# One product per cell from a crossed key plane, in the masked levels of a bidirectional gated recurrence

## The chip, the cores and the metric

The kernel runs on one core of a Trainium2 chip. The metric is the device time of one execution in microseconds (us). TensorE (PE) multiplies, VectorE (DVE) and ScalarE (ACT) work elementwise, GpSimd (POOL) does one kind of subtraction here, and SyncE (SP) issues the transfers. The engines run on their own and meet at semaphores; each takes its instructions strictly in the order in which they are written.

## What is computed

Two layers, each with a feed-forward block before and after a token mixer: the first mixer is latent attention, the second a gated linear recurrence (HGRN2) in both directions over 512 tokens with 8 heads of 128. The change is in the recurrence alone. Per head and direction the reference computes

```python
# S_t = diag(f_t) S_{t-1} + k_t outer v_t ; o_t = S_t^T q_t
diff = where(lower, bt[t] - bt[s], -inf)        # bt: running sum of log f
scores = einsum('bhtd,bhsd,bhtsd->bhts', qt, kt, exp(diff))
o = scores @ vt + einsum('bhtd,bhdv->bhtv', qt * exp(bt), state)
```

so the score of a query t and a key s is a product over 128 channels in which every channel carries the product of the gates between s and t. The two directions are summed.

## The kernel before, in words

**Levels.** The kernel does not scan. It splits the pairs (t, s) by levels m = 1, 2, 4, ..., 256: at level m the tokens stand in blocks of 2m, and a pair belongs to the level if s and t lie in different halves of one block. `k_lev` and `q_lev` (two planes each, one per direction, 128x1024 a plane for the two heads worked on together) hold keys and queries already multiplied by the gates up to the middle of their block. `update(n, m)` on DVE (L1847) brings them from level m to 2m: two products for the queries (L1852), one for the keys (L1854), whose operands `crossed` (L384) walks over the first halves of the blocks in plane 0 and the second halves in plane 1, and one that pairs up the gates (L1857).

**Masked levels.** For m = 1 to 16 the blocks are smaller than the 32x32 cells in which scores are computed. `masked(n, m)` on PE (L909) computes all 32 cells (8 columns of cells, 4 groups of 32 rows) of a level, each as two products: plane d of the keys against those queries of plane 1-d that lie in the other halves, 16 columns each (L919). All five levels write to one PSUM bank. DVE copies what belongs to the level through a mask into `nearest` (`keep`, L1861, instruction L1872). Only after that may the next level overwrite the bank.

**Quarters.** The heads go in four quarters n = 0 to 3 of two heads. While the scores of quarter n are made, the projections of the next quarter run between them. PE's written order around the masked levels is: `masked(n, 1)`, a projection (24 products of 128x512, L554 to L556), `masked(n, 2)`, a projection, and so on up to `masked(n, 16)`, a projection, `within_64` (L932, level 32, one product per cell and 32 columns). In quarters 1 and 2 (counted from 0) some small products stand there too: the sums of squares (L1005) before `masked(n, 2)`, `widen` (L651) before `masked(n, 4)` and `masked(n, 8)`. In the last quarter the output projection takes the place of the projections; it starts from `xg_hi` and `xg_lo`, which ACT (L1436) and DVE (L1892) make of the normed heads.

**DVE's written order** at a masked level of quarters 0 to 2 is: `keep`, `update(n, m)`, `evict()` (L1648, the finished projection times a norm factor into one of three temporaries), `split` (L1605, the low part of a weight tile). **ACT's written order** there is: `gate(n + 1, i)` (L1364 to L1381: four instructions L1375, L1376, L1378, L1380 on the temporary that `evict()` has just made), `hi_part()` (L1171, the high part of a weight tile, 128x1024), and the next gate. The weight tiles go through a ring of four.

The lines that matter here:

```python
# ACT, at the top of the loop over quarters
for n in range(QUARTERS - 1):
    hi_part()
    gate(n + 1, 0)
    hi_part()
    ...
    gate(n + 1, 1)
    hi_part()
# DVE
keep(0, 1)
update(0, 1)
evict()
split(s, t + 5)
keep(0, 2)
```

Of the kernel before, what the change touches and what calls it, by code (L numbers as in the profile page):

```python
# [29 lines left out]
F32 = mybir.dt.float32  # L30
# [3 lines left out]
ACT = mybir.ActivationFunctionType  # L34
ALU = mybir.AluOpType
AX = mybir.AxisListType.X

P = 128
D_MODEL, SEQ, DEPTH, D_FF = 1024, 512, 2, 2816
# [12 lines left out]
SUB = 32  # L52
# [159 lines left out]
def build(nc, x, w_up, w_down, w_mla, w_hgrn, columns, consts, positions, out):  # L212
    ctx = ExitStack()
    with ctx:
        def sb(name, shape, dt=F32):
            return ctx.enter_context(nc.sbuf_tensor(name, shape, dt))

        def sem(name):
            return ctx.enter_context(nc.semaphore(name))
# [20 lines left out]
        t_d = sb("t_d", [P, SEQ])  # L240
        cos = sb("cos", [P, SEQ])
        sin = sb("sin", [P, SEQ])
        eps = sb("eps", [P, 1])
        lb = sb("lb", [P, 2, HEADS])
        one_lb = sb("one_lb", [P, 2, HEADS])
# [119 lines left out]
        act_step = sem("act_step")  # L365
        gate_ready = sem("gate_ready")
        level_ready = sem("level_ready")
        score_done = sem("score_done")
        score_out = sem("score_out")
        near_made = sem("near_made")  # L370
# [13 lines left out]
        def crossed(both, m):  # L384

            start = both[:, 0, :]
            return bass.AP(tensor=start.tensor, offset=start.offset,
                           ap=[list(start.ap[0]), [2 * m, N // (2 * m)], [N + m, 2], [1, m]])

        def runs(n, m):  # L390

# [143 lines left out]
        def _(pe):  # L535
# [42 lines left out]
            def close(instruction):  # L578

                instruction.then_inc(w_free, 1)  # L580
                closed[0] = True
# [287 lines left out]
            def hgrn():  # L869
# [21 lines left out]
                def cell(c, g):  # L891
                    return slice(c * P + g * SUB, c * P + g * SUB + SUB)

                def of_cell(ps, c, g):
                    return ps[g * SUB:(g + 1) * SUB, c * SUB:(c + 1) * SUB]
# [13 lines left out]
                def masked(n, m, closing=False):  # L909

                    ps = open_scores()
                    pe.wait_ge(level_ready, LEVELS_UP * n + m.bit_length())
                    for c in range(CELLS):
                        for g in range(P // SUB):
                            out_c = of_cell(ps, c, g).rearrange("p (b two m) -> p b two m", two=2, m=m)
                            for d in range(2):
                                queries = q_lev[n % 2][:, 1 - d, cell(c, g)]
                                queries = queries.rearrange("p (b two m) -> p b two m", two=2, m=m)
                                last = pe.matmul(out_c[:, :, 1 - d, :], k_lev[n % 2][:, d, cell(c, g)],  # L919
                                                 queries[:, :, 1 - d, :], start=True, stop=True)  # L920
                                if closing and c == g == d == 0:
                                    close(last)
                    last.then_inc(score_done, 1)

                def within_64(n):
# [230 lines left out]
        def _(act):  # L1156
# [9 lines left out]
            def hi_part(blocks=8):  # L1166

                slot = stream.slot()
                act.wait_ge(raw_full[slot], raw_in[slot].next(16))
                n = blocks * P  # L1170
                act.activation(w_hi[slot][:, 0:n], raw[slot][:, 0:n], ACT.Copy).then_inc(hi_made, 1)  # L1171
# [184 lines left out]
            def hgrn():  # L1356
# [8 lines left out]
                def gate(n, i):  # L1365

                    d, j = i // PAIR, i % PAIR
                    at = slice(j * SEQ, (j + 1) * SEQ)
                    head = slice(n * PAIR + j, n * PAIR + j + 1)
                    z = next_temp()  # L1370
                    keys = k_lev[n % 2][:, d, at]
                    if gated.count:
                        act.wait_ge(gate_ready, gated.count)
                    gated.more += 1
                    act.activation(t_c[:, :], z, ACT.Sigmoid).then_inc(act_step, 1)  # L1375
                    act.activation(keys, z, ACT.Sigmoid, scale=-1.0).then_inc(taken, 1)  # L1376
                    act.wait_ge(taken, took.next())
                    act.activation(keys, keys, ACT.Copy, scale=one_lb[:, d, head])  # L1378
                    act.wait_ge(act_step, steps.next())
                    act.activation(gates[n % 2][:, d, at], t_c[:, :], ACT.Identity, bias=lb[:, d, head],  # L1380
                                   scale=one_lb[:, d, head]).then_inc(gate_ready, 1)  # L1381

                def query(j):
                    z = next_temp()
                    took.more += 1
                    act.activation(q_raw[:, j * SEQ:(j + 1) * SEQ], z, ACT.Silu).then_inc(taken, 1)

                def output_gate(n, j):
                    z = next_temp()
                    took.more += 1  # L1390
                    act.activation(y[:, n * PAIR + j, :], z, ACT.Silu).then_inc(taken, 1)

                def unit():
                    act.wait_ge(unit_done, units.next())
                    return psum[:, UNIT_BANKS[(units.count - 1) % 2], :]
# [5 lines left out]
                def nearest_out(n):  # L1401
                    act.wait_ge(score_out, SCORES * (n + 1))
                    for g in range(P // SUB):
                        rows = slice(g * SUB, (g + 1) * SUB)
                        last = act.activation(near[rows, :, rows], nearest[rows, :, :], ACT.Copy)
                    last.then_inc(near_made, 1)
# [26 lines left out]
                def o_hi(head):  # L1433
                    act.wait_ge(chunk_new, normed + head + 1)
                    new.more += 1
                    act.activation(xg_hi[:, head, :], y[:, head, :], ACT.Copy).then_inc(chunk_hi, 1)  # L1436
# [6 lines left out]
                hi_part()  # L1443
                query(0)
                query(1)
                hi_part()
                out_of_psum.more += PAIR
                values_out(0, 0)
# [2 lines left out]
                for n in range(QUARTERS - 1):  # L1451
                    hi_part()
                    gate(n + 1, 0)
                    hi_part()
                    if n:
                        take_root([(0, CELLS, P)], TAIL_BANKS[0])
                    gate(n + 1, 1)
                    hi_part()
                    gate(n + 1, 2)
                    hi_part()  # L1460
                    gate(n + 1, 3)
                    hi_part()
                    query(0)
                    nearest_out(n)
                    hi_part()
                    within_64_out()
                    query(1)
                    hi_part()
                    within_128_out()
                    output_gate(n, 0)  # L1470
                    hi_part()
                    within_256_out()
                    output_gate(n, 1)
                    out_of_psum.more += PAIR
                    hi_part()
                    across_out(0)
                    hi_part()
                    o_out(0)
                    across_out(1)
                    values_out(n + 1, 0)  # L1480
                    o_out(1)
                    values_out(n + 1, 1)

                n = QUARTERS - 1
                hi_part()
                output_gate(n, 0)
                hi_part()
                act.wait_ge(drained, out_of_psum.count + 1)
                o_hi(0)
                take_root([(0, CELLS, P)], TAIL_BANKS[0])  # L1490
                output_gate(n, 1)
                o_hi(1)
                o_hi(2)
                o_hi(3)
                hi_part()
                o_hi(4)
                o_hi(5)
                nearest_out(n)
                hi_part()
                hi_part()  # L1500
# [40 lines left out]
        def _(dve):  # L1541
# [283 lines left out]
            def hgrn(s):  # L1825
# [21 lines left out]
                def update(n, m):  # L1847

                    dve.wait_ge(level_ready, LEVELS_UP * n + m.bit_length())
                    for d in range(2):  # L1850
                        q = pairs(q_lev[n % 2], 1 - d, m)[:, :, 1 - d, :]
                        dve.tensor_tensor(q, q, of_runs(n, d, d, m), ALU.mult)  # L1852
                    k = crossed(k_lev[n % 2], m)
                    dve.tensor_tensor(k, k, crossed_runs(n, m), ALU.mult).then_inc(level_ready, 1)  # L1854
                    if m < P:
                        both = runs(n, m)[:, :, 0:N // m].rearrange("p d (b two) -> p d b two", two=2)
                        dve.tensor_tensor(runs(n, 2 * m)[:, :, 0:N // m // 2], both[:, :, :, 0], both[:, :, :, 1],  # L1857
                                          ALU.mult).then_inc(dve_step, 1)
                        dve.wait_ge(dve_step, step.next())
# [290 lines left out]
```

## Time and profile before

| what | value |
|---|---|
| median of 3 runs | 2126.39 us (2120.18 to 2127.16) |
| profiled execution, own time | 2123.81 us |
| its span | 2122.0 us |
| PE busy | 2077.4 us, 98% of the span |
| PE weight loads | 1703.3 us, 80% |
| DVE, ACT, POOL busy | 897.6, 690.0, 664.9 us |
| mean granted clock of PE | 0.991 |
| the recurrence's stage | about 1370 to 1720 us of the span |

Busy time of PE counts overlapping products once. An fp32 product shows as two records. A time in a row is that of the merged records, from the start of the first to the end of the last, and the last part of a product overlaps the start of the next. Intervals are therefore read from start to start below.

### The profile page before, as it was taken

To read this page: it belongs to the slowest core of one execution; us is meant where nothing else is said; L and a number is where in the kernel's file an instruction comes from. 1 tells how busy PE (TensorE), PEld (TensorE's weight loads), DVE (VectorE), ACT (ScalarE), POOL (GpSimd) and SP (SyncE) were. 2 spreads that over 40 slices of the span, in tenths; PEclk is the share of its full clock that TensorE was granted. 3 is DMA by queue.
4 is the path that set the end of the run, shared out by engine and by line. 5 is a ranking of instruction groups with operands and counts; after the bars stand their busy time and mean duration, and the time that the engine had idled before them with its cause. 6 is when DMAs were issued, how large, how long until landed. Compare 5 with 4: busy or idle time off the path is not lost.

```text
span 2122.0 us, 31462 instructions
## 1 busy us (share of the span) xinstructions
PE 2077.4 (98%) x12734; PEld 1703.3 (80%) x12734; DVE 897.6 (42%) x1223; ACT 690.0 (33%) x930; POOL 664.9 (31%) x286
## 2 busy tenths in 40 slices
PE   8999999989999999999999999999999999999997
PEld 6888888767878888887888888878888778888885
DVE  4433331668464333015433311564755756333213
ACT  4222232445342222223222222453544443222221
POOL 2444444130224444442444444200000013444442
PEclk9999999999999999999999999999999999999998
DMA  4222333210122222332222333221211112222332
GB/s 149 89 90 98 97 92 99 90 50 1 51 89 89 89 98 96 92 99 89 89 92 96 97 92 99 90 72 61 72 61 62 52 70 80 99 92 96 92 102 74
DMA packets 51643, 179.61 MB, mean 85 GB/s; under 512 B 5728, under 2 KB 5984, under 8 KB 51552
## 3 DMA queue, kind: packets, MB, share of 16 engines
q1 hardware_dynamic: 51552, 178.30, 25.9%
q8 instruction: 68, 1.11, 0.2%
q14 instruction: 23, 0.19, 0.0%
HBM read 176.18 MB, written 2.10 MB: 84 GB/s over the span
## 4 chain that ended last, share of the span: by engine, by line
PE 92%; DVE 5%; ACT 2%; issue 1%; DMA 0%; DVEq 0%; SPq 0%; ACTq 0%
PE psum L554 27%; PE psum L556 26%; PE psum L555 26%; PE psum L815 1%; PE psum L791 1%; PE psum L919 1%; PE psum L672 1%; PE psum L666 1%; PE psum L667 1%; DVE xt L1590 1%; DVE xg_lo L1596 1%; PE psum L804 1%; PE psum L968 1%; ACT xg_hi L1214 1%; PE psum L651 1%
## 5 line engine op out<-in xcount | busy, mean ns | idle before, releaser
L504 POOL TENSOR_TENSOR w_lo<-raw,w_hi 128x1024 fp32r<-128x1024 f32 (+1 forms) x282 | 664.7, 2359 | 1426.5 <-ACT w_hi L1171 1426.5
L554 PE MATMUL psum<-xg_hi,w_hi 128*128 128x512 f32 x1758 | 701.1, 399 | 10.9 <-DVE t_a L1648 4.3
L556 PE MATMUL psum<-xg_hi,w_lo 128*128 128x512 f32 x1758 | 690.9, 393 | 0.0
L555 PE MATMUL psum<-xg_lo,w_hi 128*128 128x512 f32 x1758 | 688.0, 391 | 0.0
L1171 ACT ACTIVATE w_hi<-raw 128x1024 fp32r<-128x1024 f32 (+1 forms) x339 | 350.8, 1037 | 839.5 <-DMA raw<-w_up 461.2
L554 PEld LDWEIGHTS psum<-xg_hi,w_hi 128*128 128x128 f32 x1758 | 331.9, 189 | 84.0 <-DVE t_a L1648 6.0
L556 PEld LDWEIGHTS psum<-xg_hi,w_lo 128*128 128x128 f32 x1758 | 331.6, 189 | 76.4
L555 PEld LDWEIGHTS psum<-xg_lo,w_hi 128*128 128x128 f32 x1758 | 331.8, 189 | 70.2
L554 PE MATMUL psum<-hid_hi,w_hi 128*128 128x512 f32 x704 | 273.9, 389 | 0.0
L556 PE MATMUL psum<-hid_hi,w_lo 128*128 128x512 f32 x704 | 273.9, 389 | 0.0
L555 PE MATMUL psum<-hid_lo,w_hi 128*128 128x512 f32 x704 | 273.9, 389 | 0.0
L1648 DVE TENSOR_TENSOR t_b<-psum,r_pre 128x512 f32<-128x512 f32 x100 | 69.1, 691 | 354.0 <-PE psum L556 353.3
L1669 DVE COPY y<-psum 128x512 f32<-128x512 f32 x48 | 33.2, 691 | 399.0 <-PE psum L556 341.1
L555 PEld LDWEIGHTS psum<-hid_lo,w_hi 128*128 128x128 f32 x704 | 132.1, 188 | 27.7
L556 PEld LDWEIGHTS psum<-hid_hi,w_lo 128*128 128x128 f32 x704 | 132.1, 188 | 27.4
L554 PEld LDWEIGHTS psum<-hid_hi,w_hi 128*128 128x128 f32 x704 | 132.1, 188 | 27.4
L1648 DVE TENSOR_TENSOR t_a<-psum,r_pre 128x512 f32<-128x512 f32 x100 | 69.1, 691 | 153.0 <-PE psum L556 132.9
L1655 DVE TENSOR_TENSOR t_d<-t_c,t_b 128x512 f32<-128x512 f32 x88 | 116.4, 1322 | 17.4 <-ACT t_c L1236 6.2
L1236 ACT ACTIVATE t_c<-t_a 128x512 f32<-128x512 f32 x88 | 55.7, 633 | 142.1 <-DVE t_a L1648 142.1
L1605 DVE TENSOR_TENSOR w_lo<-raw,w_hi 128x1024 fp32r<-128x1024 f32 x57 | 69.7, 1223 | 11.6 <-ACT w_hi L1171 10.4
L1659 DVE TENSOR_TENSOR hid_lo<-t_d,hid_hi 128x512 f32 (+1 forms) x88 | 69.3, 787 | 9.4
L666 PE MATMUL psum<-xg_hi,w_hi 128*128 128x512 f32 x138 | 56.2, 407 | 2.7 <-POOL w_lo L504 1.4
(198 smaller groups left out, 1581.7 us busy)
## 6 DMA issues: line engine op xcount, KB each, us to landing
raw<-w_up SPq DMA_DIRECT2D x176, 512.0 KB, 3.3
raw<-w_down SPq DMA_DIRECT2D x64, 512.0 KB, 3.5
raw<-w_hgrn SPq DMA_DIRECT2D x48, 512.0 KB, 3.4
raw<-w_down SPq DMA_DIRECT2D x32, 384.0 KB, 3.1
raw<-w_mla SPq DMA_DIRECT2D x19, 512.0 KB, 3.3
xt<-x_t SPq DMA_DIRECT2D x8, 256.0 KB, 6.6
out<-xt SPq DMA_DIRECT2D x8, 256.0 KB, 2.0
sq<-positions SPq DMA_DIRECT2D x1, 256.0 KB, 9.6
```

The costliest lines, as they stand in the source:

```text
L504: pool.tensor_tensor(w_lo[slot][:, 0:n], raw[slot][:, 0:n], w_hi[slot][:, 0:n].bitcast(F32), ALU.subtract).then_inc(w_ready, 1)
L554: first = pe.matmul(ps, w_hi[slot][:, at:at + n], hi, start=start, stop=False)
L555: pe.matmul(ps, w_hi[slot][:, at:at + n], lo, start=False, stop=False)
L556: return first, pe.matmul(ps, w_lo[slot][:, at:at + n], hi, start=False, stop=stop)
L666: first = pe.matmul(banks[g], w_hi[tiles[g]][:, at], xg_hi[:, k, :], start=k == 0, stop=False)
L1171: act.activation(w_hi[slot][:, 0:n], raw[slot][:, 0:n], ACT.Copy).then_inc(hi_made, 1)
L1236: act.activation(t_c[:, :], t_a[:, :], ACT.Silu).then_inc(silu_done, 1)
L1605: dve.tensor_tensor(w_lo[slot][:, :], raw[slot][:, :], w_hi[slot][:, :].bitcast(F32), ALU.subtract).then_inc(lo_made, 1)
L1648: dve.tensor_tensor(dst, bank(), r_pre[:, :], ALU.mult).then_inc(drained, 1)
L1655: dve.tensor_tensor(t_d[:, :], t_c[:, :], t_b[:, :], ALU.mult).then_inc(dve_step, 1)
L1659: dve.tensor_tensor(hid_lo[:, f, :], t_d[:, :], hid_hi[:, f, :].bitcast(F32), ALU.subtract).then_inc(hidden_ready, 1)
L1669: dve.tensor_copy(y[:, j, :], bank()).then_inc(drained, 1)
```

## The change

Before every masked level ACT copies the keys of both planes into one plane `k_crossed` (128x1024): first halves of the blocks from plane 0, second halves from plane 1. PE then takes one product per cell, with 32 columns of queries that walk over both planes of `q_lev` in the same manner (`crossed_cell`). PE waits for that copy (`keys_crossed`). DVE's `update` makes the keys ahead of the queries and signals them by a semaphore of their own (`keys_ready`). `k_crossed` lies where `cos` and `sin` of the attention layer were; there is one of it, and its next writing is ordered behind the products that read it. Where ACT does each copy is written out:

```diff
+        k_crossed = nc.alloc_sbuf_tensor_at("k_crossed", [P, N], F32, offset=nc.sbuf_base - 2 * SEQ * 4)
...
+        def crossed_cell(both, at, m):
+            start = both[:, 0, at]
+            return bass.AP(tensor=start.tensor, offset=start.offset,
+                           ap=[list(start.ap[0]), [2 * m, SUB // (2 * m)], [N + m, 2], [1, m]])
...
                     pe.wait_ge(level_ready, LEVELS_UP * n + m.bit_length())
+                    pe.wait_ge(keys_crossed, N_MASKS * n + m.bit_length())
                     for c in range(CELLS):
                         for g in range(P // SUB):
-                            out_c = of_cell(ps, c, g).rearrange("p (b two m) -> p b two m", two=2, m=m)
-                            for d in range(2):
-                                queries = q_lev[n % 2][:, 1 - d, cell(c, g)]
-                                queries = queries.rearrange("p (b two m) -> p b two m", two=2, m=m)
-                                last = pe.matmul(out_c[:, :, 1 - d, :], k_lev[n % 2][:, d, cell(c, g)],
-                                                 queries[:, :, 1 - d, :], start=True, stop=True)
+                            last = pe.matmul(of_cell(ps, c, g), k_crossed[:, cell(c, g)],
+                                             crossed_cell(q_lev[n % 2], cell(c, g), m), start=True, stop=True)
...
+                def cross_keys(n, m):
+                    if m > 1:
+                        act.wait_ge(keys_ready, (LEVELS_UP - 1) * n + m.bit_length() - 1)
+                    else:
+                        act.wait_ge(gate_ready, Z_TILES * (n + 1))
+                        if n:
+                            act.wait_ge(score_done, SCORES * n)
+                    act.activation(k_crossed[:, :].rearrange("p (b two m) -> p b two m", two=2, m=m),
+                                   crossed(k_lev[n % 2], m), ACT.Copy).then_inc(keys_crossed, 1)
...
                 query(1)
+                cross_keys(0, 1)
                 hi_part()
...
                 for n in range(QUARTERS - 1):
                     hi_part()
                     gate(n + 1, 0)
+                    cross_keys(n, 2)
                     hi_part()
...
                     gate(n + 1, 1)
+                    cross_keys(n, 4)
                     hi_part()
                     gate(n + 1, 2)
+                    cross_keys(n, 8)
                     hi_part()
                     gate(n + 1, 3)
+                    cross_keys(n, 16)
                     hi_part()
...
                     output_gate(n, 1)
+                    cross_keys(n + 1, 1)
...
                 output_gate(n, 0)
+                cross_keys(n, 2)
                 hi_part()
...
                 o_hi(1)
+                cross_keys(n, 4)
                 o_hi(2)
                 o_hi(3)
+                cross_keys(n, 8)
                 hi_part()
                 o_hi(4)
                 o_hi(5)
+                cross_keys(n, 16)
...
                     dve.wait_ge(level_ready, LEVELS_UP * n + m.bit_length())
+                    k = crossed(k_lev[n % 2], m)
+                    dve.tensor_tensor(k, k, crossed_runs(n, m), ALU.mult).then_inc(keys_ready, 1)
                     for d in range(2):
                         q = pairs(q_lev[n % 2], 1 - d, m)[:, :, 1 - d, :]
-                        dve.tensor_tensor(q, q, of_runs(n, d, d, m), ALU.mult)
-                    k = crossed(k_lev[n % 2], m)
-                    dve.tensor_tensor(k, k, crossed_runs(n, m), ALU.mult).then_inc(level_ready, 1)
+                        last = dve.tensor_tensor(q, q, of_runs(n, d, d, m), ALU.mult)
+                    last.then_inc(level_ready, 1)
```

## Rows read from the trace of the kernel before

**Rows 1.** The page: chain that ended last; then the chain of 1388 to 1440 us, by line.

```profile
PE 92%; DVE 5%; ACT 2%; issue 1%; DMA 0%; DVEq 0%; SPq 0%; ACTq 0%
...
by line: PE psum L554 27.3%; PE psum L556 24.8%; PE psum L555 24.8%; PE psum L919 13.0%; PE psum L905 2.7%; PE psum L995 2.1%; DVE t_d L1648 1.3%; DVE v_raw L1648 1.3%; DVE t_b L1648 1.3%; PE psum L932 1.3%; PE psum L943 1.1%; issue 0.2%
```

**Rows 2.** Groups by line, PE: output, inputs, shapes, count, busy us, mean ns, idle before.

```profile
L919 PE MATMUL psum<-q_lev,k_lev 128*32 128x16 f32 x2560 | 28.7, 186 | 0.5 <-DVE k_lev L1854 0.5
```

**Rows 3.** Timeline, all engines, levels 1 and 2 of quarter 0: start, length, engine, line.

```profile
1397.66 1.43 PE L919 MATMUL psum<-q_lev,k_lev 128*32 128x16 f32 x128
...
1399.12 0.45 DVE L1872 COPY_PREDICATED nearest<-const,psum 128x256 f32<-128x256 uint32 x1 [3.77 <-PE psum L919]
...
1400.81 2.21 DVE L1854 TENSOR_TENSOR k_lev<-k_lev,gates 128x1024 f32<-128x1024 f32 x1
...
1404.12 0.69 DVE L1648 TENSOR_TENSOR t_a<-psum,r_pre 128x512 f32<-128x512 f32 x1
...
1404.73 1.43 PE L919 MATMUL psum<-q_lev,k_lev 128*32 128x16 f32 x128
1404.84 0.63 ACT L1375 ACTIVATE t_c<-t_a 128x512 f32<-128x512 f32 x1 [4.23 <-DVE t_a L1648]
...
1406.20 0.46 DVE L1872 COPY_PREDICATED nearest<-const,psum 128x256 f32<-128x256 uint32 x1
...
1407.37 1.05 ACT L1171 ACTIVATE w_hi<-raw 128x1024 fp32r<-128x1024 f32 x1
...
1407.90 1.22 DVE L1854 TENSOR_TENSOR k_lev<-k_lev,gates_b 128x1024 f32<-128x1024 f32 x1
```

**Rows 4.** Timeline of DVE: the masked copies of levels 4, 8 and 16, quarter 0.

```profile
1413.26 0.45 DVE L1872 COPY_PREDICATED nearest<-const,psum 128x256 f32<-128x256 uint32 x1 [1.55 <-PE psum L919]
...
1420.34 0.45 DVE L1872 COPY_PREDICATED nearest<-const,psum 128x256 f32<-128x256 uint32 x1 [1.84 <-PE psum L919]
...
1427.40 0.45 DVE L1872 COPY_PREDICATED nearest<-const,psum 128x256 f32<-128x256 uint32 x1 [1.96 <-PE psum L919]
```

**Rows 5.** Timeline of ACT: what follows gates 1, 2 and 3 there.

```profile
1413.01 1.04 ACT L1171 ACTIVATE w_hi<-raw 128x1024 fp32r<-128x1024 f32 x1
...
1419.80 1.04 ACT L1171 ACTIVATE w_hi<-raw 128x1024 fp32r<-128x1024 f32 x1
...
1426.73 1.05 ACT L1171 ACTIVATE w_hi<-raw 128x1024 fp32r<-128x1024 f32 x1
```

**Rows 6.** Timeline of PE: level 32, one product per cell.

```profile
1433.01 0.76 PE L932 MATMUL psum<-q_lev,k_lev 128*32 128x32 f32 x64
```

**Rows 7.** Timeline of DVE: what waits for level 32.

```profile
1433.82 1.29 DVE L1852 TENSOR_TENSOR q_lev<-q_lev,gates_b 128x512 f32<-128x512 f32 x2 [1.39 <-PE psum L932]
```

**Rows 8.** Timeline of DVE: first and last of five masked copies, quarters 1 and 2.

```profile
1479.70 0.45 DVE L1872 COPY_PREDICATED nearest<-const,psum 128x256 f32<-128x256 uint32 x1 [8.07 <-PE psum L919]
...
1510.47 0.45 DVE L1872 COPY_PREDICATED nearest<-const,psum 128x256 f32<-128x256 uint32 x1 [1.91 <-PE psum L919]
...
1562.74 0.45 DVE L1872 COPY_PREDICATED nearest<-const,psum 128x256 f32<-128x256 uint32 x1 [8.06 <-PE psum L919]
...
1595.09 0.45 DVE L1872 COPY_PREDICATED nearest<-const,psum 128x256 f32<-128x256 uint32 x1 [1.91 <-PE psum L919]
```

**Rows 9.** Timeline of ACT: what follows gate 0 in quarter 1.

```profile
1487.94 1.04 ACT L1171 ACTIVATE w_hi<-raw 128x1024 fp32r<-128x1024 f32 x1
```

**Rows 10.** Last quarter: ACT before the output projection, DVE, and PE's wait.

```profile
1653.61 1.04 ACT L1171 ACTIVATE w_hi<-raw 128x1024 fp32r<-128x1024 f32 x1
...
1655.00 1.22 DVE L1605 TENSOR_TENSOR w_lo<-raw,w_hi 128x1024 fp32r<-128x1024 f32 x1
...
1658.33 0.79 PE L554 MATMUL psum<-xg_hi,w_hi 128*128 128x512 f32 x1 [2.34 <-DVE xg_lo L1892]
```

**Rows 11.** PE by windows: length, busy, granted clock, DMA share, GB/s.

```profile
1572.00:1574.00 2.00, 2.00 (x6) 0.50 0.60 199
...
1658.00:1660.00 2.00, 1.67 (x4) 0.50 0.95 360
```

More of the change, by code:

```diff
@@ L367, in build @@
         level_ready = sem("level_ready")
+        keys_ready = sem("keys_ready")
+        keys_crossed = sem("keys_crossed")
         score_done = sem("score_done")
@@ L912, in masked @@
                     pe.wait_ge(level_ready, LEVELS_UP * n + m.bit_length())
+                    pe.wait_ge(keys_crossed, N_MASKS * n + m.bit_length())
                     for c in range(CELLS):
                         for g in range(P // SUB):
-                            out_c = of_cell(ps, c, g).rearrange("p (b two m) -> p b two m", two=2, m=m)
-                            for d in range(2):
-                                queries = q_lev[n % 2][:, 1 - d, cell(c, g)]
-                                queries = queries.rearrange("p (b two m) -> p b two m", two=2, m=m)
-                                last = pe.matmul(out_c[:, :, 1 - d, :], k_lev[n % 2][:, d, cell(c, g)],
-                                                 queries[:, :, 1 - d, :], start=True, stop=True)
-                                if closing and c == g == d == 0:
-                                    close(last)
+                            last = pe.matmul(of_cell(ps, c, g), k_crossed[:, cell(c, g)],
+                                             crossed_cell(q_lev[n % 2], cell(c, g), m), start=True, stop=True)
+                            if closing and c == g == 0:
+                                close(last)
                     last.then_inc(score_done, 1)
```

## The prediction, made before the changed kernel ran

> **What bounds the kernel now.** I read the page's chain first: 92% of the span lies on PE, so what shortens PE's own work shortens the kernel, and what makes PE wait lengthens it. The same view cut to one quarter of the recurrence shows the masked products with 13.0% of the stretch and no ACT instruction in the chain [rows 1]. By line, the masked products keep PE busy 28.7 us in all, and PE waited 0.5 us before them [rows 2]. Then I read the engines one after the other around two levels [rows 3]: PE is never late there, DVE waits 3.77 us for the masked products, and ACT waits 4.23 us for DVE. All the gates' work on ACT is hidden. The question is whether the new copy, which PE must await, is hidden too. That depends on where it stands in ACT's order.
>
> **The product stage.** From the start of a masked level to DVE's copy out of it (K from here on: the start of L1872) pass 1399.12 - 1397.66 = 1.46 us; the second time it is 1.47 [rows 3]. That is 128 records at some 11 ns. Level 32 is already what the change makes of the others: one product per cell, 32 columns, 64 records. It takes 1433.82 - 1433.01 = 0.81 us to the DVE instruction behind it [rows 6, 7]. So each of 20 masked levels is 0.66 us shorter (1.47 - 0.81); were PE never to wait, that would be 13.2 us.
>
> The new queries' pattern costs something only at m = 1, where neighbouring elements lie in different planes. DVE's key product has just this walk: 2.21 us at m = 1, 1.22 us at m = 2 [rows 3]. For PE I bound the four m = 1 stages between 0.81 and the old 1.47 us, and take 0.81, as the stage goes by records and not by elements. The 2.6 us between (4 x 0.66) go into the range.
>
> **The copy itself.** No row shows ACT crossing planes. The nearest is ACT's copy of 128x1024, 1.05 us [rows 3]. Upper bound: DVE's ratio at m = 1, 2.21/1.22, gives 1.9 us. For m of 2 and more DVE pays nothing for the same walk, so I take 1.05. The four copies of m = 1 stand early, behind the queries or the output gate, and have until the level's turn of values is over, so they delay only weight work that DVE does ahead of need: nothing.
>
> The Trainium skill, SBUF — State Buffer, Door 1: The DMA port swizzle, says that an engine reads at full rate only if it touches a 16-byte line at least twice in a row. DVE's 2.21 against 1.22 us agrees: at m = 1 every element changes line, at m = 2 two follow each other. By this rule the copies of m = 2 to 16 cost the plain 1.05 us, and the upper end falls away for them.
>
> **The wait.** In quarters 0 to 2 the copy for level 2m stands behind `gate(n + 1, i)`. That gate reads a temporary which DVE makes behind `update(n, m)`, and that update stands behind K. The order is thus a ring: masked products, K, update, evict, gate, crossing, next masked products. In quarter 0, level 1: K at 1399.12, evict from 1404.12 to 1404.81, gate from 1404.84, and ACT free for the next thing at 1407.37, which is K + 8.25 [rows 3]. The keys have been ready for 4 us by then. With the crossing (1.05), a handover (0.03, as from 1404.81 to 1404.84) and the short stage (0.81) the next K comes 10.14 us after the last. PE alone would be back after 7.08 - 0.66 = 6.42 us. So PE stands still 3.7 us where it never waited.
>
> The other levels, the same way. K + D, with D the start of L1171 less K: 6.81, 6.54 and 6.39 us for levels 2, 4 and 8 [rows 3, 4, 5]; next K after 8.70, 8.43 and 8.28; PE waits of 2.3, 2.0 and 1.9 us. D shrinks because the gates' product (L1857) gets smaller.
>
> Sum of quarter 0: D is 27.99 in all, plus 4 x 1.89 = 7.56, makes 35.55 us. Before, from 1399.12 to 1427.40, it was 28.28 [rows 3, 4]. +7.27, and -0.66 for level 1's own stage: **+6.6 us**.
>
> Quarter 1: D is 8.24 at the first [rows 8, 9] and as above at the others within 0.07; 35.6 us in place of 30.77 [rows 8], since PE has more small work between: +4.8 - 0.66 = **+4.2 us**. The square root that ACT makes between two gates there ends before the next temporary comes, so it adds nothing. Quarter 2: 35.6 in place of 32.35 [rows 8] - 0.66 = **+2.6 us**; its 1.58 us over quarter 1 went with a granted clock of 0.50 for a while [rows 11], and a wait swallows that.
>
> Last quarter: no gates. The copy for level 2 stands before `hi_part` at 1653.61, so that ends 1.0 us later, at some 1655.7, and DVE's split at 1655.00 [rows 10] starts 0.7 late. Behind it come evict, the high and the low part, and PE, which waits for them 2.34 us already [rows 10]: +0.7. The copy for level 8 must await that level's keys and holds `hi_part` and DVE's next split by some 0.4. Stages shorten where PE or the chain from K counts: levels 1, 4 and 16, 3 x 0.66 = -2.0. Net **-0.9 us**.
>
> DVE's new order inside `update` moves no later instruction; it only brings the keys 1.2 us earlier. No transfer is moved: SP's queue waits for tiles that PE frees, as before, and the weights have a tile in hand. Behind the waiting PE instruction stands only PE's own work; DVE and ACT wait for it in the ring.
>
> **The clock.** A wait followed by small products lets the granted clock fall: 0.50 behind the 2.34 us wait of the last quarter, and 0.50 once in quarter 2, without any idle time, behind the small products [rows 10, 11]. The cost was 1.58 us there. Behind levels 1 to 8 the next wait (1.6 to 2.3 us) swallows it. Behind level 16 of three quarters nothing does: half a chance of 1.6 us each, +2.4.
>
> The Trainium skill, TensorE: Matmul & The Clock Gate, Why this matters for your kernels, warns against idle gaps between bursts of matmuls, since they put the array back to half rate. The fall behind the 2.34 us wait agrees.
>
> Sum: 6.6 + 4.2 + 2.6 - 0.9 + 2.4 = **+14.9 us**. On the profiled execution's 2123.8 us this gives 2138.7. The median of the runs lies 2.6 us above that execution, within their spread of 7 us; I take half of the difference: **2140 us**.
>
> **The rivals.**
>
> *Heavy waits.* The clock falls after each of the 12 waits and stays low for twice as long as in quarter 2: 3.2 us lost, 1.6 swallowed, 1.6 left at 9 places and 3.2 at 3, which is 24 us in place of 2.4; or the crossing takes 1.9 us after all, 12 x 0.85 = 10 us. Either gives 2150 to 2162. For it: twelve waits of about 2 us, and small products around them. Against it: in quarters 0 and 1 the present small products leave the clock alone.
>
> *Light waits.* The ring is shorter than I sum, with +1 to +7 us (2127 to 2133). For it: in quarter 1 PE's own small work is half as long as the waits. It would need ACT or DVE to run ahead in the ring, and no row shows how.
>
> *Hidden crossing, faster.* One mechanism: ACT gets to the crossing before PE gets to the stage, so PE keeps its 13.2 us: 2126 - 13 = 2113 us. It decides at K + 5.6 us, PE's return with the projection done; the copy would have to start by K + 4.5, while the gate in front of it ends at K + 8.25 [rows 3] and at K + 6.4 to 6.8 at later levels [rows 4, 5]. It would be so if the gate's temporary were made before the update. The written order says otherwise. If only 12 of the 20 stages gained and waits ate the rest, nothing would change: 2126.
>
> *The change doesn't do what it says*: 64 records take as long as 128. Then the stage stays at 1.47, and the forecast rises by some 13 us; level 32 speaks against it. It belongs to the heavy case.
>
> **How the numbers follow.** Ring as summed: 0.68. Heavy: 0.18. Light: 0.08, half of it within the noise, since some 0.3% (6 us) is what can be told from no change here. Hidden or nearly so: 0.06, of which 0.02 no change. Faster 0.04, same 0.06, slower 0.90. Range: below, no clock loss and a ring 6 us cheaper in all, 2131; above, most of the heavy case, 2157.
>
> **What would show it.** Right: 1280 records on the masked line, stages of about 0.8 us; PE waiting for ACT at the masked products some 12 times for 1.6 to 3.7 us, 25 us in all, the first of each quarter among the longest; K to K of 10.1, 8.7, 8.4, 8.3 us; no such wait in the last quarter; windows of half clock behind some waits, which take nothing while a further wait follows. Wrong: no PE wait for ACT, a copy well off 1.05 us at m of 2 and more, or half clock through whole projections.

## The result, and the profile after

The changed kernel takes 2145.9 us (median of 4 runs, 2141.4 to 2149.8) beside 2123.6 us for the kernel before: a ratio of 1.011, 95% interval 1.0088 to 1.0132. The change makes the kernel slower, by some 22 us. The forecast was 2140 us (2131 to 2157). Its profiled execution has a span of 2139.7 us, 17.7 more than before, at a mean granted clock of 0.987; its own time is 2141.4, and the other three runs took 2142.5 to 2149.8 at 0.985 to 0.981.

The waits of PE in the recurrence, longest in total first (us in total, times, longest):

```profile
PE psum L925 <- ACT k_crossed L1407: 21.0, 11, 3.9
PE psum L563 <- DVE xg_lo L1920: 6.3, 3, 3.5
...
PE psum L925 <- DVE q_lev L1881: 0.4, 1, 0.4
```

The masked products are L925 now, ACT's copy is L1407. Ten of its eleven waits are in quarters 0 to 2, one of 0.33 us is in the last. A wait that did not exist before has 21.0 us. That is more than the 12.1 us that the products gave back in busy time, as their group shows beside the old one [rows 2] (28.7 us then):

```profile
L925 PE MATMUL psum<-q_lev,k_crossed 128*32 128x32 f32 x1280 | 16.6, 208 | 21.4 <-ACT k_crossed L1407 21.0 <-DVE q_lev L1881 0.4
```

The timeline from level 1 to level 2 of quarter 0 answers to [rows 3]; first PE, then DVE, then ACT:

```profile
1396.87 0.89 PE L925 MATMUL psum<-q_lev,k_crossed 128*32 128x32 f32 x64
...
1403.08 0.40 PE L565 MATMUL psum<-xg_hi,w_lo 128*128 128x512 f32 x1
1407.35 1.08 PE L925 MATMUL psum<-q_lev,k_crossed 128*32 128x32 f32 x64 [3.87 <-ACT k_crossed L1407]
```

```profile
1397.82 0.45 DVE L1900 COPY_PREDICATED nearest<-const,psum 128x256 f32<-128x256 uint32 x1 [3.25 <-PE psum L925]
...
1402.81 0.69 DVE L1675 TENSOR_TENSOR t_a<-psum,r_pre 128x512 f32<-128x512 f32 x1
...
1408.49 0.45 DVE L1900 COPY_PREDICATED nearest<-const,psum 128x256 f32<-128x256 uint32 x1 [3.72 <-PE psum L925]
```

```profile
1403.54 0.63 ACT L1381 ACTIVATE t_c<-t_a 128x512 f32<-128x512 f32 x1 [3.71 <-DVE t_a L1675]
...
1405.35 0.80 ACT L1386 ACTIVATE gates<-t_c,lb,one_lb 128x512 f32<-128x512 f32 x1
1406.05 1.15 ACT L1407 ACTIVATE k_crossed<-k_lev 128x1024 f32<-128x1024 f32 x1
```

K is at 1397.82, the temporary is made from 1402.81, the gate starts at K + 5.72, the crossing at K + 8.23. PE had its last projection product issued at 1403.08 and stood 3.87 us. The next K comes 10.67 us after the first (forecast 10.14, before 7.08).

The later copies out (DVE L1900), the last three of quarter 0, then the first and last of quarters 1 and 2, answer to [rows 4] and [rows 8]:

```profile
1417.26 0.45 DVE L1900 COPY_PREDICATED nearest<-const,psum 128x256 f32<-128x256 uint32 x1 [3.28 <-PE psum L925]
...
1425.77 0.45 DVE L1900 COPY_PREDICATED nearest<-const,psum 128x256 f32<-128x256 uint32 x1 [3.27 <-PE psum L925]
...
1434.14 0.45 DVE L1900 COPY_PREDICATED nearest<-const,psum 128x256 f32<-128x256 uint32 x1 [3.27 <-PE psum L925]
...
1485.89 0.45 DVE L1900 COPY_PREDICATED nearest<-const,psum 128x256 f32<-128x256 uint32 x1 [7.55 <-PE psum L925]
...
1522.53 0.45 DVE L1900 COPY_PREDICATED nearest<-const,psum 128x256 f32<-128x256 uint32 x1 [3.27 <-PE psum L925]
...
1575.88 0.45 DVE L1900 COPY_PREDICATED nearest<-const,psum 128x256 f32<-128x256 uint32 x1 [7.55 <-PE psum L925]
...
1612.50 0.46 DVE L1900 COPY_PREDICATED nearest<-const,psum 128x256 f32<-128x256 uint32 x1 [3.27 <-PE psum L925]
```

K to K in quarter 0: 10.67, 8.77, 8.51 and 8.37 us, where 10.14, 8.70, 8.43 and 8.28 were forecast. From first to last K it is 36.32 us (28.28 before), 36.64 (30.77) and 36.62 (32.35) in the three quarters.

Windows of the first wait and what follows (length; busy time of PE, its weight loads, DVE, ACT, POOL; granted clock, DMA share, GB/s):

```profile
1404.00:1406.00 2.00, 0.00 (x0) 0.00 (x0) 0.76 (x1) 1.97 (x4) 0.00 (x0) 1.00 0.00 0
1406.00:1408.00 2.00, 0.65 (x49) 0.68 (x53) 0.00 (x0) 2.00 (x3) 0.00 (x0) 0.67 0.00 0
1408.00:1410.00 2.00, 2.00 (x37) 1.65 (x28) 1.48 (x2) 0.15 (x1) 0.00 (x0) 0.50 0.03 8
1410.00:1412.00 2.00, 2.00 (x7) 1.52 (x6) 2.00 (x4) 0.00 (x0) 0.00 (x0) 0.50 0.86 252
1412.00:1414.00 2.00, 2.00 (x7) 1.63 (x6) 1.92 (x2) 1.21 (x3) 0.00 (x0) 0.63 0.03 10
```

PE is at 1.2 GHz, its lower level, for about 6 us behind the wait: the masked stage itself lasts 1.08 us in place of 0.75, and the projection behind it runs slow. The fall began while PE still waited. Level 2 of quarters 1 and 2 shows the same, with waits of 2.28 us and stages of 1.08. Behind level 16 the clock fell in quarter 1 alone:

```profile
1524.00:1526.00 2.00, 2.00 (x6) 1.55 (x5) 1.97 (x5) 0.00 (x0) 0.00 (x0) 0.50 0.72 248
```

In the last quarter PE's waits for the heads' low parts (2.34 us before [rows 10]) are longer:

```profile
1676.10 0.79 PE L563 MATMUL psum<-xg_hi,w_hi 128*128 128x512 f32 x1 [3.48 <-DVE xg_lo L1920]
1687.07 0.80 PE L563 MATMUL psum<-xg_hi,w_hi 128*128 128x512 f32 x1 [1.97 <-DVE xg_lo L1920]
```

```profile
1672.76 1.23 DVE L1632 TENSOR_TENSOR w_lo<-raw,w_hi 128x1024 fp32r<-128x1024 f32 x1 [0.90 <-ACT w_hi L1177]
```

### The profile page after: what moved, and what is told of

The parts are those of the page before. It is cut to its first block, busy times and chain, and to the rows that moved or that the text cites. A ratio compares the mean times of both kernels' runs of the same rounds, so it can differ in the third digit from the quotient of the medians.

```text
span 2139.7 us, 28925 instructions
## 1 busy us (share of the span) xinstructions
PE 2072.0 (97%) x11454; PEld 1695.1 (79%) x11454; DVE 920.4 (43%) x1223; ACT 711.5 (33%) x950; POOL 664.9 (31%) x286
## 4 chain that ended last, share of the span: by engine, by line
PE 87%; DVE 6%; ACT 4%; issue 2%; DMA 0%; DVEq 0%; SPq 0%; ACTq 0%
PE psum L563 25%; PE psum L564 25%; PE psum L565 25%; PE psum L824 1%; PE psum L800 1%; PE psum L681 1%; DVE xt L1617 1%; PE psum L676 1%; PE psum L675 1%; DVE q_lev L1881 1%; DVE xg_lo L1623 1%; PE psum L925 1%; PE psum L813 1%; ACT k_crossed L1407 1%; PE psum L974 1%
## 5 line engine op out<-in xcount | busy, mean ns | idle before, releaser
L1682 DVE TENSOR_TENSOR t_d<-t_c,t_b 128x512 f32<-128x512 f32 x88 | 137.4, 1561 | 17.4 <-ACT t_c L1242 6.2
```

What stands on the lines that cost most here:

```text
L1682: dve.tensor_tensor(t_d[:, :], t_c[:, :], t_b[:, :], ALU.mult).then_inc(dve_step, 1)
```

## The experiments

Each was timed in turn with the kernel before on the same chip. Where a difference to the changed kernel is given, it is to 2146.1 us, its median in e0. The experiments ran in three groups at different times and on different chips: e0 to e3, then e4, e5, e6 and e8, then e7 and e9. The kernel before had medians of 2121.5, 2123.2 and 2121.9 us in the three, so a difference across groups is uncertain by 1 to 2 us from this alone.

**e0: the changed kernel again.** No edit.

> The changed kernel once more, beside the kernel before and the other experiments, since the runs of both kernels spread over 7 to 8 us. Theory (the ring masked products, copy out, update, evict, gate, crossing, next masked products): about 18 to 22 us above the kernel before, with 12 waits of PE for the crossing in quarters 0 to 2, of 1.6 to 3.9 us.

2146.1 us (2140.4 to 2148.9), ratio 1.0111 (1.0097 to 1.0125), 24.6 us above the kernel before. The five runs line up by their mean granted clock: 2140.4 us at 0.987, 2146.0 and 2146.1 at 0.984, 2148.6 at 0.983, 2148.9 at 0.982. PE's waits for the crossing are 21.3 us here and 21.0 in the faster profile above: the waits do not make the spread. Of the 7.1 us between the two profiled executions of the changed kernel (spans of 2146.8 and 2139.7) half lie ahead of the recurrence: the first masked products start at 1400.49 us here and at 1396.87 there, where the two run the same instructions (the clock over 400 to 500 us is 0.93 and 0.98). The rest is 0.7 us in the rings, 1.2 behind level 16, 1.2 in the last quarter and 0.4 after it.

**e1: the copy ahead of the gate.**

```diff
-                    gate(n + 1, 0)
                     cross_keys(n, 2)
+                    gate(n + 1, 0)
...
-                    gate(n + 1, 1)
                     cross_keys(n, 4)
+                    gate(n + 1, 1)
```

and the same for gates 2 and 3.

> ACT's crossing for levels 2, 4, 8 and 16 of quarters 0 to 2 stands ahead of the gate instead of behind it; nothing else differs from the changed kernel. Ring theory: the keys are there at K + 1.7 (K + 2.7 at level 1), so the crossing ends at K + 3 to 4, before PE is back at K + 5.6; no wait for the crossing is left, and the saving of the product stages shows: about 12 us below the kernel before, near 2111, some 30 us below the changed kernel. Rival (the cost is in the crossed queries' pattern or in 20 copies of 1.05 us on ACT, wherever they stand): still 10 us or more above the kernel before. Rival (the cost is mostly the granted clock): the clock falls are tied to PE's waits, so they would go as well; half clock in windows around masked levels 2 to 16 would remain under the pattern rival only.

2114.4 us, ratio 0.9962 (0.9948 to 0.9975): 31.7 us below the changed kernel and 7 below the kernel before, by four pairs of lines changing places. The waits of PE in the recurrence:

```profile
PE psum L563 <- DVE xg_lo L1920: 6.3, 3, 3.5
...
PE psum L925 <- ACT k_crossed L1407: 0.3, 1, 0.3
```

The same 20 copies and the same crossed patterns are in it, so neither is the cost. Over 1388 to 1640 us the granted clock is 0.96 in the changed kernel and 1.00 here; the falls went with the waits. The gain is smaller than the 12 us expected. The twelve levels of quarters 0 to 2 did give what was summed: 81.8 us from first to last K in the three quarters together, where e7, which has the old products, has 89.8, so 8.0 for 12 x 0.66. The stages of m = 1 gave 0.5 us each. The last quarter took some of it back: 30.5 us from first to last K, where e7 has 27.9. e8 looks into that.

**e2: copies and waits, old products.**

```diff
-                            last = pe.matmul(of_cell(ps, c, g), k_crossed[:, cell(c, g)],
-                                             crossed_cell(q_lev[n % 2], cell(c, g), m), start=True, stop=True)
+                            for d in range(2):
+                                ...
+                                last = pe.matmul(out_c[:, :, 1 - d, :], k_lev[n % 2][:, d, cell(c, g)],
+                                                 queries[:, :, 1 - d, :], start=True, stop=True)
```

> The copies, the waits and the orders of the changed kernel, but the products are the old ones: two per cell, 16 columns each, read from the keys' two planes; the crossed plane is written and awaited but not read. Ring theory: the stage is part of the ring in every level, so the saving of 0.66 us is gone at 19 to 20 levels: 12 to 13 us above the changed kernel, near 2157, and K to K of 10.8, 9.4, 9.2, 9.0 us in quarter 0. Rival (the product stage is hidden behind the wait, and only the wait counts): the same time as the changed kernel. Rival (the one-product form is itself slow): faster than the changed kernel.

2159.4 us, ratio 1.0176 (1.0162 to 1.0190), 13.3 us above the changed kernel (12 to 13 expected). So the shorter stage does pay, also behind a wait: it is a link of the ring. Where the masked stages ran at the full clock in both, a level is 0.66 us longer (level 4 to level 8 of quarter 1: 9.23 in place of 8.57); where it had fallen, 0.86 (level 1 to level 2 of quarter 0: 11.53 in place of 10.67). That the total met the expectation is in part luck: in its profile the three rings together are 13.7 us longer (123.3 and 109.6), where 12 x 0.66 is 7.9, at a clock of 0.93 over 1388 to 1640 us and with 4.6 us in which PE waited for nothing that the profile shows. The copies and waits without the shorter stage cost 38 us against the kernel before.

**e3: the temporary ahead of the update.** ACT's order is the changed kernel's.

```diff
                 keep(0, 1)
-                update(0, 1)
                 evict()
+                update(0, 1)
```

and so for levels 2, 4 and 8, and in the loop over quarters.

> ACT's order is the changed kernel's, with the gate ahead of the crossing; on DVE the temporary that the gate reads is made (evict) ahead of update for levels 1 to 8. Ring theory: the gate starts at K + 1.2 and ends at K + 3.8, the crossing ends at K + 4.9, before PE is back at K + 5.6; the waits go although ACT's order is untouched, and the time is near 2111 to 2114, as in the version with the copy ahead of the gate. Rival (it is the length of ACT's work between two masked levels, gate and copy and weight part, that does not fit): ACT's work per level is the same, so the time would stay at 18 to 22 us above the kernel before.

2113.1 us, ratio 0.9957 (0.9944 to 0.9971). ACT does the same work in the same order, and the waits are gone (0.3 us left). It is not how much ACT has to do between two levels but what its gate waits for.

**e4 and e5: every copy twice**, in the changed kernel and in e1.

```diff
                     act.activation(k_crossed[:, :].rearrange(...), crossed(k_lev[n % 2], m),
-                                   ACT.Copy).then_inc(keys_crossed, 1)
+                                   ACT.Copy).then_inc(act_step, 1)
+                    act.wait_ge(act_step, steps.next())
+                    act.activation(k_crossed[:, :].rearrange(...), crossed(k_lev[n % 2], m),
+                                   ACT.Copy).then_inc(keys_crossed, 1)
```

> The changed kernel with every crossing made twice, one behind the other. Ring theory: the second copy (some 1.05 to 1.25 us with its wait for the first) lies on the ring at the 12 places of quarters 0 to 2, so 12 x 1.15 = 14 us above the changed kernel, near 2160, and PE's waits for the crossing grow from 21 to some 33 to 36 us. Rival (PE's waits come from the level's keys on DVE or from the gate alone): within 3 us of the changed kernel.

> Every crossing made twice, in the version with the copy ahead of the gate. Ring theory: the second copy ends at K + 4 to K + 5.2, still before PE is back at K + 5.6, and the gate, whose temporary comes at K + 3.9 to 5.7, starts hardly later: within 4 us of that version with one copy (2114), where the last quarter pays some of it. Rival (20 copies on ACT cost their own length wherever they stand): 20 x 1.15 = 23 us above 2114.

e4: 2164.1 us, ratio 1.0187 (1.0167 to 1.0207), 18 us above the changed kernel (14 expected). PE's waits:

```profile
PE psum L925 <- ACT k_crossed L1410: 35.9, 15, 5.1
```

35.9 us in place of 21.0, within what was expected. In the profile the three rings together are 124.0 us, 14.4 more than after the change, which is the 14 expected. What is beyond it went with the clock, 0.978 to 0.983 in its runs: from the last K of a quarter to the next K pass 54.1 us in all three quarters, where the changed kernel has 51.8, 53.4 and 51.8, and the level 16 stages ahead of them take 1.08 us. The last quarter is 3.6 us longer. e5: 2115.5 us, ratio 0.9968 (0.9957 to 0.9980), 1.1 us above e1. A copy costs its length where it is in the ring, and next to nothing outside it.

**e6 and e9: the waits filled with constant products.**

```diff
+FILL = ({2: 13, 4: 8, 8: 7, 16: 6}, {2: 7, 4: 6, 8: 5, 16: 6})
...
+                    if n + 1 < QUARTERS and m > 1:
+                        for _ in range(FILL[n > 0][m]):
+                            pe.matmul(psum[:, MASKED_BANK, 2 * P:4 * P], const[:, 0:P], const[:, 0:2 * P], start=True, stop=True)
                     pe.wait_ge(keys_crossed, N_MASKS * n + m.bit_length())
```

> The changed kernel with products of constants (128x256, 6 to 13 of them, results not used) put on PE between the projection and the masked products of levels 2 to 16 of quarters 0 to 2, so that PE is busy where it would wait; they are meant to last about as long as the wait. Ring theory: the waits shrink to nothing and the ring's length stays, so only what the granted clock costs comes back: 3 to 6 us below the changed kernel, near 2141, half clock gone from quarters 0 to 2, and the spread of its runs less than 8 us. Rival (the clock costs nothing, since the next wait swallows it): no change, or some us slower where the fill is longer than the wait.

e6: 2147.5 us, 1.4 above the changed kernel (24.3 above the kernel before of its own group, where e0 has 24.6). The fill was too long: its first stretch (26 records) lasts 5.78 us for a wait of 3.9, and first K to last K became 40.3, 38.6 and 38.5 us, 7.8 more in all than after the change. A ring 7.8 us longer and a median only 1.4 us longer suggest that some 6 us came back elsewhere, but its profile shows 1.6 of them: no fall is left behind level 16 (51.7 us from the last K of a quarter to the next in all three). This was the slowest of the four runs, 2153.0 us beside 2146.3 to 2148.2, and it reached the first masked products 3.8 us later than the changed kernel's profile, at 1400.67. The shorter fill is e9:

> As the version with filled waits, with fewer constant products (9, 5, 5, 4 in quarter 0, then 5, 4, 4, 4), since the first fill was longer than the wait (K to K 12.0, 9.9, 9.4, 9.0 us in quarter 0, in place of 10.7, 8.8, 8.5, 8.4) and yet cost only 1.4 us in all. One fill product lasts 0.445 us. Ring theory with a clock that costs: the fill no longer lengthens the ring, the clock stays up in quarters 0 to 2, and the time falls 4 to 7 us below the changed kernel's 2146, to 2139 to 2142, with waits of PE for the crossing of under 0.6 us each. Rival (the clock costs nothing there and the first fill was not really too long): 2146 to 2148 again.

e9: 2141.7 us (2139.7 to 2144.9), ratio 1.0098 (1.0082 to 1.0113), 4.3 us below the changed kernel at the medians. The two ratios' intervals overlap, and the runs of both kernels spread over more than this, so the step is at the edge of what can be told. Its waits, and the windows over quarters 0 to 2, first of e9, then of the changed kernel:

```profile
PE psum L915 <- issue: 2.0, 2, 1.1
...
PE psum L929 <- ACT k_crossed L1411: 1.1, 5, 0.3
```

```profile
1388.00:1640.00 252.00, 249.41 (x2724) 207.19 (x2711) 148.69 (x190) 128.12 (x179) 0.00 (x0) 1.00 0.20 64
```

```profile
1388.00:1640.00 252.00, 230.00 (x2616) 190.37 (x2617) 148.68 (x190) 129.06 (x179) 0.00 (x0) 0.96 0.20 62
```

PE is busy 249 of 252 us in e9 and the kernel is hardly better off: 20 us above the kernel before. A busy PE on the chain is no sign of a good kernel. The rings are 35.8, 36.0 and 36.0 us, 1.7 less in all than after the change (36.3, 36.6, 36.6): with the clock up the first stage of a quarter behind a wait takes 0.77 us and not 1.08. The ring itself stays, and with it most of the loss. This profile shows no fall behind level 16, but PE stood still for 2.0 us there (L915) at full clock, for nothing that the profile shows, so the 4.3 us may be less than the clock costs.

**e7: keys ahead of the queries, alone**, in the kernel before.

> The kernel before with one edit alone: update makes the keys ahead of the queries. Every theory here says that DVE's later instructions do not move: within 2 us of the kernel before. If it were slower, some of the changed kernel's cost would lie in that edit.

2121.1 us, ratio 0.9998 (0.9988 to 1.0008): that edit costs nothing.

**e8: e1 with two copies moved in the last quarter.**

```diff
-                output_gate(n, 0)
                 cross_keys(n, 2)
+                output_gate(n, 0)
                 hi_part()
...
                 o_hi(3)
-                cross_keys(n, 8)
                 hi_part()
+                cross_keys(n, 8)
```

> The version with the copy ahead of the gate, and in the last quarter the copy for level 2 ahead of the output gate and the copy for level 8 behind the weight's high part. Ring theory with my reading of the last quarter: there the copy for level 2 held DVE's split by 0.9 us and the copy for level 8 held the next high part, and PE's two waits for the low parts of the heads were 3.5 and 2.0 us in place of 2.3 and 0.7; both go back nearly to that, 2 to 3 us below the version with the copy ahead of the gate alone, near 2112, and so 9 to 11 us below the kernel before. Rival (these two waits come from the masked stages being shorter, not from the copies): the same time as that version.

2112.2 us (2110.0 to 2115.1), ratio 0.9953 (0.9940 to 0.9967): 2.3 us below e1, in another group, so this step is at the edge of what can be told. In its profile PE's two waits for low parts are 3.00 and 1.40 us, where e1 has 3.48 and 1.97 and the kernel before 2.34 and 0.70. The first K of the quarter, and the first of the waits:

```profile
1634.69 0.45 DVE L1900 COPY_PREDICATED nearest<-const,psum 128x256 f32<-128x256 uint32 x1 [7.55 <-PE psum L925]
...
1645.68 0.80 PE L563 MATMUL psum<-xg_hi,w_hi 128*128 128x512 f32 x1 [3.00 <-DVE xg_lo L1920]
```

From this K to the end of the wait pass 10.99 us here, 11.85 in e1 (1635.65 to 1647.50) and 10.97 in the kernel before (1647.36 to 1658.33). So the delay by the copy for level 2 is gone whole. The wait is still 0.66 us longer than before because PE's stage is 0.66 us shorter: PE comes earlier to the same moment, which costs nothing. The second wait is 0.70 longer than before in the same manner. So both readings in the expectation hold in part: the copies made the low parts late, and the shorter stages made PE early. e8 beats both kernels, by 11 and some 34 us.

## Why the prediction was right, and where its sizes were off

**The ring.** Right, and shown from both ends: taking the gate out of it on ACT (e1) or the temporary's late place on DVE (e3) removes the waits, and lengthening the copy (e4) or the stage (e2) lengthens each turn. The order on each engine, read from the code, and the durations in rows gave each level of quarter 0 within 0.1 us except the first. Ten waits stand in quarters 0 to 2 where twelve were forecast, and 21.0 us where 25 were: at level 4 of quarters 0 and 2 the slow projection ate the wait, as the prediction says of the clock.

**Terms of the sum, in the profiled execution.** For each quarter, the gain of K to K less what level 1's own stage gave back (0.5 us each, not 0.66: 1.46 us became 1397.82 - 1396.87 = 0.95, then 1.01). Quarter 0: 8.0 - 0.5 = +7.5 (forecast 6.6). Quarter 1: 5.9 - 0.5 = +5.4 (4.2). Quarter 2: 4.3 - 0.5 = +3.8 (2.6). That is 3.3 us more. In it are: the handover from ACT to PE, 0.15 us (1406.05 + 1.15 = 1407.20 to 1407.35) in place of 0.03, which was read from DVE to ACT, a handover of another kind, 12 x 0.12 = 1.4 us; and the first wait's copy (1.15 in place of 1.05) and slow stage (1407.35 to 1408.49 = 1.14 in place of 0.81), 3 x 0.43 = 1.3 us; and the 0.15 us that level 1's stage gave back less, three times.

**The last quarter.** Forecast -0.9, measured +0.1 (29.30 us from first to last K in place of 28.65, less 0.5). The delay by the first copy was right: PE's first wait for a low part ends 11.84 us behind K in place of 10.97, 0.9 where 0.7 was forecast. The second wait grew by 1.3 us, from 0.70 to 1.97, but half of that is PE coming 0.66 us earlier: e2, with the old stages and this copy in place, waits 1.31, so the copy for level 8 cost 0.6 where 0.4 was forecast. What the sum lacked is a fall of the clock behind that second wait: 0.51 over 1688 to 1690 us, and 6.49 us from the end of the wait to the last K, where e3, with the same wait of 1.97 and the clock at 1.00, has 5.15. The prediction counted falls behind level 16 alone.

**The clock.** The term that was mis-sized most. I put +2.4 us in: half a chance of 1.6 us behind level 16 of three quarters, and nothing behind levels 1 to 8, on the ground that the next wait swallows a fall. It does swallow the slow projection, but not the masked stage that runs slow in the ring, and nothing swallows the fall in the last quarter. In the profile above I can name 4.6 us: 1.7 in the rings (by e9's shorter ones), 1.6 behind level 16 (from the K of level 16 to the next masked products 50.77, 50.74 and 50.74 us before; 50.74, 52.34 and 50.74 after) and 1.3 in the last quarter. The kernel before had falls too, one of 1.6 us in its quarter 2, which the prediction took as gone behind a wait.

The terms then meet the profile: 14.9, and 3.3 more in the rings, 1.0 more in the last quarter, 0.8 less behind level 16, and 0.8 less because this execution reached the first masked products at 1396.87 and not at 1397.66, make 17.6, and 17.7 was measured.

At the medians the change costs 22 and 25 us, 5 to 7 more than in that profile, whose run was the fastest of its four. Not all of this is clock behind waits: e0's profile has 3.6 us of it ahead of the recurrence, and e7's, of a kernel without the copies, has the same late start (1400.57). e9 gives 4.3 us for the falls in quarters 0 to 2, at the edge of what can be told. What share each has at the medians was not separated and stays open.

**The base.** I started from the profiled execution (2123.8) and half of the way to the median of three runs. With more runs the kernel before is at 2121.5 to 2123.6, and my base was 2125.1, so it was 2 to 4 us high, which by luck hid part of the error in the difference: 15 us were forecast, and 22 to 25 measured.

**The rivals.** Hidden crossing: its condition was the right one. Made true in e3 by the temporary ahead of the update, as the prediction said, it takes the waits away. That e3's 2113.1 us meet the 2113 of this rival is luck: it took 13 us from 2126, and the runs show 8.4 from 2121.5. Heavy waits: partly true through the clock, and not through the copy, which takes 1.04 to 1.19 us at m of 2 and more. Copies twice as long would have given about what e4 shows. One product per cell taking as long as two: false, 0.75 us for 64 records against 1.43 for 128.

**The rule on lines.** The copy at m = 1 takes 1.53 us, at m = 2 1.15, and from m = 4 on 1.04 (quarters 0 to 2). The Trainium skill, SBUF — State Buffer, Door 1: The DMA port swizzle, asks for two accesses to each 16-byte line for full rate; m = 1 agrees, and m = 2 pays 0.11 us although it has two. For PE, the m = 1 stage lasts 0.89 us against 0.75.

## What to carry to other kernels

When a new step takes its input from engine A and is awaited by engine C, write down what stands ahead of it in its own engine's order, and what that waits for; if this leads back to C, the step closes a ring, and every link of it adds to the time at every turn, however idle the engines look. Here the place of four lines was worth 32 us of 2146, more than twice the whole gain that the change was able to bring. A stage can be bounded from a neighbour that already has the new form (level 32 gave 0.81 us for what became 0.79), but a handover has to be read between the same two engines.

## What the runs showed of the hardware that was not expected

A wait of 3.87 us left the granted clock at 0.50 for about 6 us behind it, and a masked stage of 64 records then took 1.08 us in place of 0.75. The fall began before the wait had ended. It was no matter of long waits only: the waits of 2.28 us at level 2 of quarters 1 and 2 were followed by the same 1.08 us stages. The same wait of 1.97 us in the last quarter was followed by a clock of 0.51 in one profile and of 1.00 in another (e3). Filling the waits with products of no use brought the clock from 0.96 back to 1.00 over quarters 0 to 2, made the three rings 1.7 us shorter in all, and went with a median 4.3 us lower, at the edge of what can be told.

Within one group, runs line up by their mean clock, those of the kernel before as well (2115.7 us at 0.994 and 2123.9 at 0.990 beside e9). The five runs of e0 spread over 8.5 us where nine of the kernel before spread over 3.4, but the kernel before spread over 7.0, 7.6 and 8.2 us in its other groups. So it is not shown that the change widens the spread.
